# GLA core: exponents' arguments as products of log gates with 0/1 matrices, and one modulation round in the SSD scan instead of the GLA core

## The reference, cut to what matters

```python
logit = jnp.einsum('blzr,zrd->zbld', a.reshape(b, l, 2, GLA_RANK), w_a2) + b_a2[:, None, None, :]
log_a = jax.nn.log_sigmoid(logit.astype(jnp.float32)) / GLA_GATE_NORM
...
cum = jnp.cumsum(gi, axis=2)
diff = cum[:, :, :, None, :] - cum[:, :, None, :, :]
decay = jnp.exp(jnp.where(mask, diff, -jnp.inf))
attn = jnp.einsum('bhid,bhjd,bhijd->bhij', qi, ki, decay)
o = jnp.einsum('bhij,bhjv->bhiv', attn, vi) + jnp.einsum('bhid,bhdv->bhiv', qi * jnp.exp(cum), s)
last = cum[:, -1:, :]
s_new = s * jnp.exp(last[:, :, 0, :, None]) + jnp.einsum('bhjd,bhjv->bhdv', ki * jnp.exp(last - cum), vi)
...
m_l = jnp.split((s_lat @ ada_w[i] + ada_b[i])[:, None, :], 6, axis=-1)
```

## Time and profile before

| | us |
|---|---|
| median of 3 runs | 2659.57 (2659.36 to 2666.67) |
| the profiled execution | 2668.94 |
| its span in the trace | 2667.2 |
| GLA projection, from the end of the front stage | about 52 to 204 |
| GLA core | 204.1 to 370.9 |
| the SSD scan's groups | 1074 to 1174 |

### The profile page before, as it was taken

One profiled execution on the slowest core, in us unless ns is written; L12 is line 12 of the kernel. 1 busy time (PEld: TensorE's weight loads), 2 busy tenths in 40 slices (PEclk: granted clock), 3 DMA queues, 4 the chain that ended last, 5 costly groups with the idle time before them and its releaser, 6 DMA issues. The chain is left out here.

```text
span 2667.2 us, 35079 instructions
## 1 busy us (share of the span) xinstructions
PE 2481.5 (93%) x13744; PEld 1969.8 (74%) x13744; DVE 1360.4 (51%) x2129; ACT 1195.9 (45%) x2029; POOL 617.8 (23%) x376
## 2 busy tenths in 40 slices
PE   5997889999998998999997999999999979999988
PEld 3784457888888888578996767577767858768778
DVE  2207657433445666347665534552566444454665
ACT  1833334422327433455554345564366234565363
POOL 1437620000006434110001442003301116403310
PEclk8998999999999999988998999999999989999999
DMA  7236852333324332645764231222222323334333
GB/s 229 79 87 210 294 171 79 112 96 94 102 72 135 103 87 64 243 152 149 199 188 112 63 93 46 68 57 75 72 65 71 87 64 95 108 91 116 86 102 114
DMA packets 416683, 302.12 MB, mean 113 GB/s; under 512 B 10306, under 2 KB 388776, under 8 KB 416520
## 3 DMA queue, kind: packets, MB, share of 16 engines
q1 hardware_dynamic: 415408, 299.45, 38.3%
q10 hardware_dynamic: 1112, 0.44, 0.1%
HBM read 298.80 MB, written 1.05 MB: 112 GB/s over the span
## 5 line engine op out<-in xcount | busy, mean ns | idle before, releaser
L207 POOL TENSOR_TENSOR weights_lo<-wslots,weights_hi 128x1024 fp32r<-128x1024 f32 x158 | 386.6, 2455 | 868.7 <-ACT weights_hi L197 622.3
L197 ACT ACTIVATE weights_hi<-wslots 128x1024 fp32r<-128x1024 f32 x398 | 418.2, 1054 | 292.7 <-PE psum L260 235.0
L260 PE MATMUL psum<-input_hi,weights_hi 128*128 128x512 f32 (+1 forms) x1400 | 501.0, 358 | 4.5 <-PEq L831 1.8
L260 PE MATMUL psum<-input_hi,weights_lo 128*128 128x512 f32 (+1 forms) x1400 | 489.1, 349 | 0.0
L260 PE MATMUL psum<-input_lo,weights_hi 128*128 128x512 f32 (+1 forms) x1400 | 488.3, 349 | 0.0
L207 DVE TENSOR_TENSOR weights_lo<-wslots,weights_hi 128x1024 fp32r<-128x1024 f32 x240 | 296.4, 1243 | 187.7 <-ACT weights_hi L197 187.4
L260 PEld LDWEIGHTS psum<-input_hi,weights_hi 128*128 128x128 f32 x1400 | 264.5, 189 | 44.7 <-issue 7.5
L260 PEld LDWEIGHTS psum<-input_lo,weights_hi 128*128 128x128 f32 x1400 | 263.4, 188 | 39.2 <-issue 3.4
L260 PEld LDWEIGHTS psum<-input_hi,weights_lo 128*128 128x128 f32 x1400 | 263.7, 188 | 38.1
L260 PE MATMUL psum<-ffn_hidden_hi,weights_hi 128*128 128x512 f32 (+1 forms) x512 | 172.8, 338 | 0.0
L260 PE MATMUL psum<-ffn_hidden_hi,weights_lo 128*128 128x512 f32 (+1 forms) x512 | 172.5, 337 | 0.0
(11 more groups left out here) (449 smaller groups left out, 4864.7 us busy)
## 6 DMA issues: line engine op xcount, KB each, us to landing
wslots<-w_in SPq DMA_DIRECT2D x132, 512.0 KB, 3.9
wslots<-ffn_w SPq DMA_DIRECT2D x128, 512.0 KB, 4.1
wslots<-ada_w SPq DMA_DIRECT2D x96, 512.0 KB, 4.9
wslots<-ssd_w_in SPq DMA_DIRECT2D x49, 512.0 KB, 4.0
wslots<-w_ada SPq DMA_DIRECT2D x48, 512.0 KB, 4.6
wslots<-gla_w_in SPq DMA_DIRECT2D x25, 512.0 KB, 3.8
wslots<-w_br SPq DMA_DIRECT2D x24, 512.0 KB, 3.6
wslots<-ssd_w_out SPq DMA_DIRECT2D x16, 512.0 KB, 4.8
```

The costliest lines, as they stand in the source:

```text
L197: act.activation(self.part(self.whi_r, n), self.slot(n), ACT.Copy)\
L207: engine.tensor_tensor(self.part(self.wlo_r, n), self.slot(n), self.part(self.whi, n), ALU.subtract)\
L260: ins = pe.matmul(out_of(self.bank(g)), l, r, start=first and i == 0, stop=last and i == len(pairs) - 1, skip_group_check=not (first and l ...
```

## The change

The projection now makes the logits token-major, with the bias as a 33rd row of the weights against a row of ones; Abs reads the bank, and VectorE writes the log gate to the free half of `h2`, with no running sum. VectorE also builds, from two constant masks, `gla_sums`: per direction nine 0/1 matrices of 128 x 128, whose product with a chunk's log gates is the argument of each of the nine exponentials (seven levels, key hat, query hat).

In the core the log gates of a head are rounded by ScalarE and split by VectorE into high and low part, in the space of the weight ring. TensorE makes the arguments: per head three groups of three matrices, each in eight fills (four chunks, two directions, one bank per direction) of two matmuls with 384 columns. ScalarE takes one exponential per fill, into `gla_decay`. `make_diff`, `factors` and `hats` are gone. VectorE makes both sides of a level, k's and q's, in two multiplications by an access pattern that crosses from one to the other; GpSimd keeps the query hats and the bias of the vectors. The order on TensorE is written out anew, with pieces of `arguments` between the other work; they run one group ahead.

Round 5 moves from the core to the SSD scan: 32 steps in the core, 32 in the scan, where each of the four heads of a group now has one.

```diff
-ADA_ROUND = {"ada_front": 0, "ada_core": 1, "ada_scan": 6}
+ADA_ROUND = {"ada_front": 0, "ada_core": 1, "ada_scan": 5}
-    ada("ada_core", [1, 2, 3, 4, 5])
+    ada("ada_core", [1, 2, 3, 4])
-    ada("ada_scan", [6, 7, 8])
+    ada("ada_scan", [5, 6, 7, 8])
...
-                    act.activation(lx[:, n % 2, :], b.psum[:, 4 + n % 4, :], ACT.Identity,
-                                         bias=column(b, C_GLAB, n)).then_inc(b.tick("logit_read"), 1)
...
-                        ins = dve.tensor_tensor_scan(cum[:, 0, h, :], reset[:], le[:, n % 2, :], 0.0,
-                                                     ALU.mult, ALU.add)
...
+                    dve.scalar_tensor_tensor(b.H2[:, n, :], b.psum[:, 4 + n % 4, :], 0.0, le[:, n % 2, :],
+                                             ALU.min, ALU.subtract).then_inc(b.tick("log_gate_made"), 1)
...
+                def arguments(G, first, last):
...
+                    for i in range(first, last):
+                        c, z = divmod(i, 2)
+                        f = G * FILLS + i
+                        if f >= 2:
+                            pe.wait_ge(b.sem("exponents_taken"), b.nth("exponents_taken", f - 1))
+                        for part, side in enumerate((gates_hi_r, gates_lo_r)):
+                            ins = pe.matmul(b.psum[:, ARG[z], 0:WIDE * P], side[:, z * CH + c, h * GDK:(h + 1) * GDK],
+                                            sums_r[:, z, g * WIDE * P:(g + 1) * WIDE * P], start=part == 0, stop=part == 1)
+                        ins.then_inc(b.tick("arguments_made"), 1)
...
+                for h in range(GH):
+                    G = h * GROUPS
+                    arguments(G + 1, 0, 2)
+                    if h:
+                        scores(h, 0)
+                    arguments(G + 1, 2, 4)
+                    if h:
+                        vectors(h, 0, 0, 1)
+                        outputs(h - 1)
+                    arguments(G + 1, 4, 6)
+                    scores(h, 1)
+                    if h:
+                        vectors(h, 0, 1, STEPS[h][0])
+                    arguments(G + 1, 6, 8)
+
+                    arguments(G + 2, 0, 1)
+                    scores(h, 2)
+                    turn_keys(h, 0)
+                    arguments(G + 2, 1, 3)
+                    vectors(h, 1, 0, STEPS[h][1])
...
-        STEPS = [1, 1, 1, 2, 2, 2, 1]
+        STEPS = [(2, 1, 1, 1, 2, 1, 1)] * 2 + [(2, 1, 1, 1, 1, 2, 1), (2, 1, 1, 1, 0, 0, 0)]
...
+                    for i in range(first, last):
+                        c, z = divmod(i, 2)
+                        act.wait_ge(b.sem("arguments_made"), b.nth("arguments_made", G * FILLS + i + 1))
+                        act.activation(decay[:, G % 2, z, :, c * P:(c + 1) * P],
+                                       b.psum[:, ARG[z], 0:WIDE * P].rearrange("p (n k) -> p n k", k=P), ACT.Exp, scale=INV)\
+                            .then_inc(b.tick("exponents_taken"), 1)
...
+                round_gates(0)
+                exponents(0, 0, FILLS)
...
+                    exponents(G + 1, 4, 8)
+                    if h == 0:
+                        round_gates(1)
+                        round_gates(2)
+                        round_gates(3)
+                    exponents(G + 2, 0, 3)
...
+                def make_sides(h, n):
...
+                    for z in range(2):
+                        dve.wait_ge(b.sem("exponents_taken"), b.nth("exponents_taken", (G + 1) * FILLS - 1 + z))
+                        x = decay[:, G % 2, z, level_slot(n), :].rearrange("p (n i s) -> p n i s", i=2, s=s)
+                        dve.tensor_tensor(crossed(sides[:, q % 2], z, s), x, crossed(qk[:, h], z, s), ALU.mult)\
+                            .then_inc(b.tick("sides_ready"), 1)
...
-        GROUP_STEPS = 3
+        GROUP_STEPS = 4
```

More of the change, by code:

```diff
@@ L1053, in gla_layer @@
         oT = qk[:].rearrange("p h a t -> p (h a) t")
-        gla_project(b, qT, kT, v, gate, cum)
-        gla_core(b, qT, kT, v, cum, oT, stat)
+        gla_project(b, qT, kT, v, gate, sums)
+        gla_core(b, qk, v, sums, oT, stat)
         gla_out(b, oT, gate, stat)
@@ L1064, in add_squares, with gla_project @@
     ins.then_inc(b.tick("square_added"), 1)
-def gla_project(b, qT, kT, v, gate, cum):
+def gla_project(b, qT, kT, v, gate, sums):
     d = b.dram
@@ L1071, in gla_project @@
         input_parts(b, st)
[L1072 to L1076, removed]
+        RB = 2 * GRANK
+        aT = b.sb(st, "gla_a", [RB + 1, T])
+        wa = b.sb(st, "gla_wa", [RB + 1, 2, GH * GDK])
+        le = b.sb(st, "gla_le", [P, 2, GH * GDK])
+        NS = len(LEVELS)
+        pairs = b.sb(st, "gla_pairs", [P, 2, NS, P])
+        runs = b.sb(st, "gla_runs", [P, 6, P])
+        blocks = b.sb(st, "gla_blocks", [P, NS, P])
+        early = b.sb(st, "gla_early", [P, NS + 1])
+        sums_r = sums[:].bitcast(F32R)
         with b.stage() as block:
@@ new lines, in _ @@
+                low, high = slice(0, P // 2), slice(P // 2, P)
+                dve.wait_ge(b.sem("pairs_in"), b.nth("pairs_in", 32))
+                step(dve.memset(early[low, 0:1], 1.0))
+                step(dve.memset(early[high, 0:1], 0.0))
+                step(dve.tensor_reduce(early[:, 1:NS + 1], pairs[:, 0], op=ALU.add, axis=AX_X))
+                step(dve.tensor_tensor(pairs[:, 1], pairs[:, 0], pairs[:, 1], ALU.add))
+                step(dve.tensor_tensor(past, above, b.ident[:], ALU.subtract))
@@ new lines, in _ @@
+                step(dve.tensor_tensor(short, upto, b.ident[:], ALU.subtract))
+                step(dve.tensor_copy(blocks[:, NS - 1, :], b.ident[:]))
+                settle()
+                step(dve.tensor_scalar(early[:, 1:NS + 1], early[:, 1:NS + 1], 0.5, None, ALU.is_ge))
+                step(dve.tensor_tensor(cross0, past, upto, ALU.subtract))
+                step(dve.tensor_tensor(cross1, above, short, ALU.subtract))
+                for n in range(NS - 2, -1, -1):
+                    step(dve.tensor_tensor(blocks[:, n, :], blocks[:, n + 1, :], pairs[:, 1, n + 1, :], ALU.add))
+                    settle()
@@ new lines, in _ @@
+                for z, cross, rest in ((0, cross0, upto), (1, cross1, short)):
+                    step(dve.scalar_tensor_tensor(sums_r[:, z, 0, :], cross, early[:, 0:1], rest, ALU.mult, ALU.add))
+                    for n in range(NS):
+                        step(dve.scalar_tensor_tensor(pairs[:, 0, n, :], cross, early[:, n + 1:n + 2], rest, ALU.mult, ALU.add))
+                    settle()
+                    step(dve.tensor_tensor(sums_r[:, z, 3:GLA_SLOTS, :], pairs[:, 0], blocks[:], ALU.mult))
+                    settle()
@@ L1200, in gla_core @@
+                for z, slot, run, u, t in ((0, 1, past, high, low), (0, 2, upto, low, high),
+                                           (1, 1, short, low, high), (1, 2, above, high, low)):
+                    step(dve.tensor_copy(sums_r[:, z, slot, :], run))
+                    settle()
+                    step(dve.tensor_copy(sums_r[u, z, slot, t], b.ones[u, t]))
+def gla_core(b, qk, v, sums, oT, stat):
     d = b.dram
     INV = 1.0 / GATE_NORM
-    SIZES = [P // 2] + LEVELS
+    SIZES = GLA_SIZES
@@ L1342, in _, with sum_squares, vectors @@
-                addends(GH - 1, 2)
-                ada_turn(b, pe, "ada_core", 4, TURNED)
+                def sum_squares(h):
+                    pe.wait_ge(b.sem("output_copied"), b.nth("output_copied", 2 * h + 2))
+                    pe.wait_ge(b.sem("tile_squared"), b.nth("tile_squared", 2 * h + 2))
+                    add_squares(b, pe, SHARED[1], sq)
+                def vectors(h, n, first, last):
+                    for i in range(first, last):
+                        ada_step(b, pe, "ada_core", sum(map(sum, STEPS[:h])) + sum(STEPS[h][:n]) + i, ADA)
```

416 lines of the change are left out of this document (215 added, 201 removed).

## The result

The changed kernel takes 2688.52 us (median of 13 runs, 2675.28 to 2697.74); the kernel before, beside it, 2665.04 us (13 runs, 2656.21 to 2677.45). The ratio is 1.0086 with a 95% interval of 1.0067 to 1.0104: slower by about 23 us, by more than the 0.3% bound of the prediction, and outside its range (2650 to 2680). The profiled execution took 2691.1 us with a span of 2689.3, against 2667.2 before.

The account below looks back on a forecast made before the run. It took TensorE, 93% busy, as the overall bound, with no engine saturated in the core and TensorE's order limiting the scan. Core -1.9, scan +7, projection zero made +5.1 on the 2659.57 median: 2664.7, stated as 2665.0 us; range 2650 to 2680.

Parts of the forecast that it names:

- The failed step: SSD scan, moved round: DMA's 8 slots per group at 1.5 us make the period 11.8 us; scan +7 us, ends +4 and +11.
- In the core DMA falls from 80 slots to 64, 96 us: hidden.: GLA core: with the round moved out, the remaining 64 weight slots take DMA 96 us, hidden behind other work.
- So about 10 us per head are slack of TensorE: GLA core, old head 1 or 2: 27.7 us of TensorE work in 37.5; the new arguments go into the slack.
- the ring of dependent work: Old GLA core: difference, exponential, product with q or k, score, take; each link late for the next, besides DMA waits.
- The core's sum: GLA core, four heads: +2.1 + 0.9 + 1.5 - 6.4 = -1.9 us, ends -14 and +9.
- The exponentials: GLA core, ScalarE: 384 columns of PSUM take 0.5 us, between that and 0.4; 17 us per head, not the bound.
- Head 0: GLA core's first head: level 1 scores near 223.6, pause some 6 us, 5 us added for clock; 47.2 against 45.1, +2.1.
- Rival (b): Fills stall TensorE on two PSUM banks, 0.58 instead of 0.35: core +9, scan +9, total 2677.6 us; chance 0.3.
- Rival (a): Core's clock stays at 2.4 GHz in its first head, level-1 stall covered: core -14, scan +5, total 2650.6; chance 0.2.
- Rival (c): SSD scan: the moved round is free, its steps filling waits that stand there now; total 2657.7 us; chance 0.05.
- The projection: GLA projection before the core: removed evacuations and scans, added matrices and constants; zero change, 3 us if the cover fails.
- First group and one more turn: SSD scan: first group +2.3 us, as only four slots are loaded ahead; one more turn +0.5 us.

## Why the prediction was wrong, point by point

**The failed step** is "The DMA must bring 8 slots per group; when TensorE stands waiting for them in the core they come 1.5 us apart, so 11.8 us per group. That, not TensorE, is next late." It took the greater of two rates, TensorE's 11.6 and the DMA's 11.8. Those are bounds that hold for a ring deep enough. With four slots the time is TensorE's work plus what the round trip leaves uncovered, 14.13. The term was +7 and measured +20; its upper end (+11) was built from a dearer slot, 1.6 us, and not from a missing one. Its arithmetic was off as well: the two rows are 1.51 us apart, 12.1 us for eight slots and not 11.8, and 1.6 us per slot gives +11 in the seven periods alone, +14 with the first group and the turn. Neither reaches +20. Seven slots gave 11.74: the rate was right and was not the limit.

**The same error in the core**: "In the core DMA falls from 80 slots to 64, 96 us: hidden." Again bytes over rate. In the changed kernel 8.8 us of waits of the weight loads remained, with a clock drop behind the longest, and half the bytes gave 9 us back.

**"So about 10 us per head are slack of TensorE"** put the blame on the ring of dependent work and read the earlier trace rows, 33 us of waits for weights, as a symptom. The kernel with more slots shows the reverse: those waits were the slack (29 us of 167); the chain shows only below them, at 137 to 139 us. A head without them takes 31 us, 62.1 for heads 1 and 2 together, next to 27.7 of counted TensorE work. Read as the bound, they would have shown that a round taken out of the core frees far more than its eight steps, and that the arguments then have to be paid.

**The core's sum** missed by less than its reasons deserved: -1.9 forecast, +2.6 measured. It came near by luck, as two errors cancelled: a round less freed 18 us, and the arguments took 20. Head by head its pieces were sound where nothing waited for weights: heads 47.2, 38.7, 38.7, 40.3 forecast; 45.2, 38.2, 38.9, 38.0 with half the bytes. With the whole change head 2 (43.3) is off; without waits for weights it is back at 38.9.

**The exponentials** take 489 ns, in my 0.4 to 0.5. The Trainium skill (ScalarE: Activation LUTs, section What ACT_TABLE_LOAD costs) gives an estimate of 506 ns for 384 columns; the row, 489 ns, agrees within 4%.

**Head 0**: first scores of level 1 at 222.30, forecast 223.6; pause of 5.5 us, forecast about 6. The granted clock was low between 220 and 228 us (0.53 and 0.62) and back at full after, so the low stretch was shorter than the 17 us of before. The likeness to the pauses before was misread: in the kernel before TensorE stood idle for 2.75 us ahead of the drop at 211 us, not for 6.

**Rival (b)**, fills that stall TensorE, occurred where head 0 opens (7 of the 17 waits of weight loads for exponentials, 3.7 of 11.4 us, by pairs of fills 1.20 us apart, 0.60 per fill against the 0.58 of its working) and was small after. Its total, 2677.6, lay nearest, for a wrong reason. **Rival (a)** needed a lasting clock in head 0; it fell. **Rival (c)**, a free round, is what the core shows and the scan denies.

**The projection** changed by -0.9 us, forecast 0. **First group and one more turn** of the scan, +2.3 and +0.5, are not seen: the first addition is 0.2 us later, with a core that ended 1.7 later. From the last addition to the end, 1.5 us more were lost, less than the profiled executions differ by.

**The four checks named ahead**: heads 1 and 2 at 38 to 39.5 (39.6 and 43.3: no, the first by little), level 1 near 223 (yes), 40 us for head 3 (39.4, yes), additions 11.8 apart with a DMA share above 0.95 (14.13 and 0.85: no). The last one, read together, says it: slower than the rate and yet not saturated was here a ring that is too short.

## What to carry to other kernels

Before moving transfers into a stage, work out the ring's round trip: the work that the consumer does between asking for a slot and needing it must cover the landing time, here 5.0 us for 512 KB. "The DMA's rate suffices" is not enough when the consumer is in order. The Trainium skill (DMA: Bandwidth & Descriptors, section Rules for kernel authors) says to issue a DMA early and to wait on its semaphore late, so that its fixed setup cost overlaps. No run here prices the setup cost by itself. What the runs show is that the ring's depth decides how early a DMA can be issued: five slots for four were worth 12 us in the scan.

Waits for DMA on the engine that bounds a stage are the first thing to price, by giving them slots or halving their bytes, before a redesign uses "slack" that is made of them. In this kernel four idle buffers of h2 in the core and a fifth slot in the scan gave 1.4%, most of it in the core, and the redesign cost 0.9%.

A total that does not move may be two terms of 20 us. The moved round alone looked neutral.

## What the runs showed of the hardware

- A transfer of 512 KB landed in 5.0 us with four slots in the scan, one of 256 KB in 3.0. With seven slots in flight it was about 6.1, while the rate rose to 363 GB/s: more in flight makes each later and all together faster.
- Four products of a modulation step that run alone take 1.05 us, eight on all four column groups 1.06: a slot that comes late costs the overlap of the halves too.
- The rate in the core rose from 257 to 312 GB/s with eight slots for the same 80 transfers, though the page's DMA share had read 0.75 before: a share of three quarters hid 29 us of waiting.
- A pause of TensorE of some 5 us came with the lower of its two clocks (1.2 GHz, granted share 0.5) wherever it stood: at 217 to 222 us in the changed kernel, at 225 to 229 with the later splits. Shifting the pause shifted the clock's fall with it. It also fell without such a pause: with the high part alone at about 211 us, behind fills with gaps of 0.2 to 0.4 us.
- Open: how much of the 21 to 23 us that the arguments cost is TensorE's products and how much the clock and waits they bring. The run without the low parts changes both at once.
